# Latent attention of a two-block model: queries and keys projected straight into feature-major layout, only the rotary parts transposed

## The chip, the cores and the metric

One core of a Trainium2 chip runs the whole kernel. The metric is the device time of one execution in microseconds (us). Before the change the median of three runs is 1034.88 us (1034.77 to 1035.86).

## What is computed

The program is two transformer blocks on 256 tokens of width 1024, each with a mixer and a squared-ReLU MLP of width 4096; the second block has two layers. All weights are streamed once. The change touches one part, the latent attention of the last layer:

```
q_full = heads(rmsnorm(c_q, q_norm) @ w_uq, 8, 64 + 32)        # c_q: 256 x 384, w_uq: 384 x 768
q_nope, q_rope = q_full[..., :64], rope(q_full[..., 64:], positions)
kv_full = heads(rmsnorm(c_kv, kv_norm) @ w_ukv, 8, 64 + 64)    # c_kv: 256 x 256, w_ukv: 256 x 1024
k_nope, v_d = kv_full[..., :64], kv_full[..., 64:]
k_rope = rope(k_r[:, :, None, :], positions)[:, :, 0, :]       # one rotated key part for all 8 heads
s = (q_nope . k_nope + q_rope . k_rope) * 96 ** -0.5           # per head, then mask, softmax, @ v_d
```

The scores are a product over 96 features, so queries and keys must lie with their features on the partitions: `qTm[0:96, head, token]` and `kTm[0:96, head, token]`, rows 0 to 63 unrotated and rows 64 to 95 rotated.

## The kernel before, in words

The order on every engine is written out by hand, with semaphores between engines. TensorE (PE) runs each job's units one after the other; a unit is one weight tile of 128 x 1024 values that SyncE loads. ScalarE (ACT) rounds each unit to fp32r (`whi`, function `hi`, L1229) and VectorE (DVE) subtracts to get the rest (`wlo`, function `lo`, L1718), six units ahead of their use. A product is three matmuls, hi x hi, hi x lo and lo x hi (`three`, L445 to L447). PSUM has eight banks: jobs alternate between the pairs 0-1 and 2-3, and banks 4 to 7 (`W0` to `W3`) serve transposes and attention. A job may start only when the pair that it reuses has been emptied (`pair_free`, L470).

Jobs are of kinds. In kind "T" the activations are the stationary operand and the weights move, up to 512 columns at a time, and the result is token-major (tokens on the partitions). In kind "F" the weights are stationary and 256 tokens move, and the result is feature-major.

The stage in question has 24 units, numbered u = 0 to 23 in three loops that run in step: on PE (from L1158), on ACT (`for u in range(n3)`, L1623) and on DVE (L2344). The jobs are `sq` and `sk` (u 0 to 7), `cq` (8 to 11), `ckv` (12 to 14), `sv` (15 to 18), and then those of the latent attention:

- `uq0` (u = 19, 20) and `uq1` (u = 21): the queries, 512 and 256 columns wide, token-major, evicted by ACT into `qtk`;
- `kn` (u = 22): the unrotated keys, token-major, evicted into `kfl`, and `vn` (u = 23): the values.

Between them PE runs the last steps of another attention (`sb_sums` at L1114, `sb_values` at L1127). DVE rotates the key part in `ckt` at u = 20 and copies it eight times into `kfl` (L2404), and rotates the queries in `qtk` at u = 21 (`rotate`, L2331). PE then transposes all of `qtk` and `kfl`, per head and block of 128 tokens, in `mla_turn` (L1144, the transpose at L1153): eight transposes after u = 22, eight in the middle of u = 23, and sixteen behind it. ACT evicts each half of the heads with `ml_copy` (L1616 to L1620), 96 rows by 1024 columns, into `qTm` and `kTm`. After the loop, `out_job("wob", ...)` (L1007) interleaves the output projection with the steps of the latent attention: `out_part` 0 for the first token block, then the step (3, -1), which waits for `ml_T` (L1060 to L1062) and issues the first logits (`att_logits`, L651), then `out_part` 0 for the second block, and so on. The steps wait for one another through the softmax on DVE (L1803, L1806) and ACT (L1298). The last MLP follows.

ACT's order from u = 20 is: `sb_second(3)`, `hi(26)`, eviction of `uq0`; `sb_hi` twice, `hi(27)`, eviction of `uq1`; `hi(28)`, eviction of `kn`; `hi(29)`, `ml_copy(0)`, `ml_copy(1)`, eviction of `vn`; `ml_copy(2)`, `ml_copy(3)`; `hi(30)`. (The numbers are those of the stage's units; the code writes `base + u + LEAD`.) DVE's is: `lo(26)`, rotation of the key part and its copies; `sb_split` twice, `lo(27)`, rotation of the queries; `lo(28)`; `lo(29)`; and then the first step of the softmax.

## Time and profile before

| what | value |
|---|---|
| median of three runs | 1034.88 us |
| the profiled execution, its own time | 1035.65 us |
| its span in the trace | 1033.9 us |
| mean granted TensorE clock | 0.998 |
| PE busy | 1024.7 us, 99% of the span |
| DVE, ACT busy | 719.9 us (70%), 580.8 us (56%) |
| mean DMA rate | 179 GB/s |

The profile's page lists busy time per engine and the chain of work that ended last. The timelines list the instructions of one engine in order of time: start, duration, engine, line, operation, output and inputs, and in brackets the idle time before and what ended it. A matmul's duration is longer than its distance to the next one, because matmuls overlap; what counts for PE is the distance from start to start. PEld is PE's weight load, which runs beside the matmuls.

### The profile page before, as it was taken

Reading aid. Unit: us, or ns where it says so; the run is one execution under the profiler, and the core shown is the slowest. Engines: PE = TensorE matmul, PEld = TensorE weight load, DVE = VectorE, ACT = ScalarE, POOL = GpSimd, SP = SyncE. Lnnn points to the kernel's source line nnn. Section 1 sums busy time; section 2 is a strip of 40 time slices with the busy share of each in tenths; the row PEclk is TensorE's granted clock in tenths of the full one; section 3 lists DMA queues with packets and bytes.
Section 4 is the critical chain, followed back from the end, with each engine's and each line's share of the span. In section 5 each row is a group of like instructions: output and inputs, shape, how many; then the busy total and the mean of one; then the engine's idle time right before and its main releaser. Section 6 shows DMA issues by size and latency. Waiting matters only on the chain.

```text
span 1033.9 us, 16294 instructions
## 1 busy us (share of the span) xinstructions
PE 1024.7 (99%) x5808; PEld 878.3 (85%) x5808; DVE 719.9 (70%) x1156; ACT 580.8 (56%) x871; POOL 1.0 (0%) x8
## 2 busy tenths in 40 slices
PE   9999999999999999999999999999999999999997
PEld 8998888888888888888878888888998878888886
DVE  6898768787866556678676766665678669565663
ACT  6655675764654444464665544544569757444542
POOL 0000000000000000000000000000000000000000
PEclk9999999999999999999999999999999999999999
DMA  8855445464665667547324765665455336665541
GB/s 277 273 191 184 143 146 193 153 202 162 205 202 193 193 186 238 166 156 252 123 85 144 241 195 181 193 192 193 129 179 170 116 123 216 207 206 185 183 142 41
DMA packets 53846, 184.96 MB, mean 179 GB/s; under 512 B 6000, under 2 KB 9504, under 8 KB 53792
## 3 DMA queue, kind: packets, MB, share of 16 engines
q1 hardware_dynamic: 52736, 183.17, 54.4%
q10 hardware_dynamic: 1056, 1.06, 0.3%
q8 instruction: 35, 0.57, 0.2%
q14 instruction: 19, 0.16, 0.0%
HBM read 183.14 MB, written 1.07 MB: 178 GB/s over the span
## 4 chain that ended last, share of the span: by engine, by line
PE 95%; DVE 2%; DMA 1%; ACT 1%; issue 0%; SPq 0%; ACTq 0%; DVEq 0%
PE ps L445 18%; PE ps L446 18%; PE ps L447 18%; PE ps L923 15%; PE ps L926 8%; PE ps L487 3%; PE ps L563 3%; PE ps L490 2%; PE ps L898 2%; PE ps L651 1%; DMA raw<-stream 1%; PE ps L675 1%; PE ps L901 1%; DVE wlo L1718 1%; ACT whi L1229 0%
## 5 line engine op out<-in xcount | busy, mean ns | idle before, releaser
L1718 DVE TENSOR_TENSOR wlo<-raw,whi 128x1024 fp32r<-128x1024 f32 x338 | 409.8, 1222 | 157.7 <-ACT whi L1229 154.7
L1229 ACT ACTIVATE whi<-raw 128x1024 fp32r<-128x1024 f32 x338 | 353.1, 1056 | 176.2 <-PE ps L447 121.0
L445 PE MATMUL ps<-whi,y_hi 128*128 128x512 f32 (+1 forms) x524 | 206.3, 394 | 0.0
L446 PE MATMUL ps<-wlo,y_hi 128*128 128x512 f32 (+1 forms) x524 | 203.6, 389 | 0.0
L447 PE MATMUL ps<-whi,y_lo 128*128 128x512 f32 (+1 forms) x524 | 203.6, 389 | 0.0
L923 PE MATMUL ps<-hT,whi 128*128 128x512 f32 x696 | 173.8, 392 | 0.0
L923 PEld LDWEIGHTS ps<-hT,whi 128*128 128x128 f32 x696 | 126.3, 189 | 23.4
L447 PEld LDWEIGHTS ps<-whi,y_lo 128*128 128x128 f32 x524 | 98.4, 188 | 20.6
L445 PEld LDWEIGHTS ps<-whi,y_hi 128*128 128x128 f32 x524 | 98.5, 188 | 19.2 <-issue 0.5
L446 PEld LDWEIGHTS ps<-wlo,y_hi 128*128 128x128 f32 x524 | 98.6, 188 | 18.5
L926 PEld LDWEIGHTS ps<-hT,wlo 128*128 128x128 f32 x696 | 94.9, 190 | 6.8
L926 PE MATMUL ps<-hT,wlo 128*128 128x256 f32 x696 | 97.0, 282 | 0.0
L445 PE MATMUL ps<-whi,hT 128*128 128x512 f32 (+3 forms) x248 | 94.2, 380 | 0.1
L447 PE MATMUL ps<-whi,hT 128*128 128x512 f32 (+3 forms) x248 | 92.6, 373 | 0.0
L446 PE MATMUL ps<-wlo,hT 128*128 128x512 f32 (+3 forms) x248 | 92.6, 373 | 0.0
L1491 ACT ACTIVATE arena<-ps 128x512 f32<-128x512 f32 x48 | 28.5, 595 | 67.6 <-PE ps L926 67.5
L2151 DVE TENSOR_TENSOR arena<-ps,arena 128x512 f32<-128x512 f32 x48 | 33.2, 691 | 43.0 <-ACT arena L1491 43.0
L445 PE MATMUL ps<-hT,whi 128*128 128x256 f32 x192 | 55.4, 288 | 0.0
L445 PEld LDWEIGHTS ps<-whi,hT 128*128 128x128 f32 x248 | 46.6, 188 | 9.3 <-DVE wlo L1883 0.8
L446 PE MATMUL ps<-hT,whi 128*128 128x256 f32 x192 | 54.3, 283 | 0.0
L447 PE MATMUL ps<-hT,wlo 128*128 128x256 f32 x192 | 54.3, 283 | 0.0
L447 PEld LDWEIGHTS ps<-whi,hT 128*128 128x128 f32 x248 | 46.6, 188 | 7.9
(279 smaller groups left out, 1139.3 us busy)
## 6 DMA issues: line engine op xcount, KB each, us to landing
raw<-stream SPq DMA_DIRECT2D x338, 512.0 KB, 4.2
x<-x_in SPq DMA_DIRECT2D x2, 512.0 KB, 4.1
arena<-scratch ACTq DMA_DIRECT2D x1, 1024.0 KB, 10.7
arena<-rb SPq DMA_DIRECT2D x1, 1024.0 KB, 6.3
bm<-decay SPq DMA_DIRECT2D x1, 1024.0 KB, 6.5
out<-arena SPq DMA_DIRECT2D x2, 320.0 KB, 2.2
cst<-const SPq DMA_DIRECT2D x1, 520.0 KB, 7.7
raw<-stream SPq DMA_DIRECT2D x2, 256.0 KB, 5.2
```

Of the source, the lines that this page charges most:

```text
L445: pe.matmul(o, a[0], b[0], start=start, stop=False)
L446: pe.matmul(o, a[0], b[1], start=False, stop=False)
L447: return pe.matmul(o, a[1], b[0], start=False, stop=stop)
L487: pe.matmul(o, whi[:, u % RING, kt * P:(kt + 1) * P], hTw[:, kt, :], start=kt == 0, stop=False)
L490: m = pe.matmul(o[:, 0:S], wlo[:, u % RING, kt * P:(kt + 1) * P], hT[0][:, kt, :], start=False, stop=kt == KT - 1)
L563: return pe.transpose(o, i, cst[0:n, C_ID:C_ID + n])
L923: pe.matmul(o, whi[:, slot, kt * P:(kt + 1) * P], hTw[:, kt, :], start=kt == 0, stop=False)
L926: m = pe.matmul(o[:, 0:S], wlo[:, slot, kt * P:(kt + 1) * P], hT[0][:, kt, :], start=False, stop=kt == KT - 1)
L1229: act.activation(whi[:, u % RING, :], raw[:, u % RAW, :], ACT.Copy).then_inc(sem("hi_done"), 1)
L1491: act.activation(crossed[:, half % 2, :, :], ps[:, b:b + 2, S:2 * S], ACT.Copy).then_inc(sem("m_cross"), 1)
L1718: dve.tensor_tensor(wlo[:, u % RING, :], raw[:, u % RAW, :], whi[:, u % RING, :].bitcast(F32), ALU.subtract).then_inc(sem("lo_done"), 1)
L2151: dve.tensor_tensor(v, ps[:, b:b + 2, 0:S], crossed[:, half % 2, :, :], ALU.add).then_inc(sem("m_sum"), 1)
```

## The change

Three things are rearranged. The query projection is split into its rotated columns (`uqr`, 256 columns, token-major, u = 19) and its unrotated ones (`uqn`, 512 columns, u = 20 and 21). `uqn` and `kn` are of a new kind "N": the weights are stationary and 256 tokens move, so that they come out feature-major in four blocks of 128 features; block g holds head g in rows 0 to 63 and head g + 4 in rows 64 to 127. ACT evicts such a job in two instructions (`evac_heads`), rows 0 to 63 and rows 64 to 127, both into rows 0 to 63 of `qTm` or `kTm`. The 32 transposes of `mla_turn` go. In their place `rope_turn`, between u = 22 and u = 23, makes two transposes of `ckt` and four of `qtk` with the rotated parts; from these, ACT copies two of four row groups into rows 64 to 95 of `qTm` at u = 23, and DVE, behind `lo(29)`, copies the key part into one head, spreads it to the other seven, and copies the other two row groups. DVE's eight-fold copies at u = 20 go, and so do the four `ml_copy`. The first logits wait for `ml_T` 3 (one signal of ACT, two of DVE) and for the eviction of `kn`. The number of units, and what each loads, stays 24; `uqr` takes one where `uq1` took one, `uqn` two where `uq0` took two.

```diff
--- before.py
+++ after.py
@@ -54,8 +54,8 @@
 
     def add(name, kind, cols, nkt):
         nonlocal u, pair
-        kpu = KT if kind == "F" else min(nkt, UNIT // cols)
-        n = cols // P if kind == "F" else -(-nkt // kpu)
+        kpu = {"F": KT, "N": UNIT // (nkt * P)}.get(kind) or min(nkt, UNIT // cols)
+        n = cols // P // (kpu if kind == "N" else 1) if kind in "FN" else -(-nkt // kpu)
         jobs[name] = dict(kind=kind, cols=cols, nkt=nkt, kpu=kpu, u0=u, n=n, pair=pair % 2)
         u += n
         pair += 1
@@ -83,8 +83,8 @@
     pair += 2
     mlp(1)
     for name, kind, cols, nkt in (("sq", "F", 512, KT), ("sk", "F", 512, KT), ("cq", "T", 384, KT),
-                                  ("ckv", "T", 288, KT), ("sv", "T", 512, KT), ("uq0", "T", 512, 3),
-                                  ("uq1", "T", 256, 3), ("kn", "T", 512, 2), ("vn", "T", 512, 2)):
+                                  ("ckv", "T", 288, KT), ("sv", "T", 512, KT), ("uqr", "T", 256, 3),
+                                  ("uqn", "N", 512, 3), ("kn", "N", 512, 2), ("vn", "T", 512, 2)):
         add(name, kind, cols, nkt)
     jobs["wob"] = dict(kind="O", u0=u, n=8, pair=pair % 2)
     u += 8
...
@@ -503,6 +503,14 @@
                         if mid is not None and kt == KT // 2:
                             mid()
                         m = three(o, wsl(u, kt * P, (kt + 1) * P), X(kt), kt == 0, kt == KT - 1)
+                elif j["kind"] == "N":
+                    nkt = j["nkt"]
+                    for i in range(j["kpu"]):
+                        block = k * j["kpu"] + i
+                        o = ps[:, b + block // 2, (block % 2) * S:(block % 2 + 1) * S]
+                        for kt in range(nkt):
+                            c = (i * nkt + kt) * P
+                            m = three(o, wsl(u, c, c + P), X(kt), kt == 0, kt == nkt - 1)
                 else:
                     w = j["cols"]
                     kts = range(k * j["kpu"], min((k + 1) * j["kpu"], j["nkt"]))
@@ -1059,7 +1067,8 @@
                         pe.wait_ge(sem("evac_v"), evac_v_no["fk"])
                     if (a, n) == (3, -1):
 
-                        pe.wait_ge(sem("ml_T"), 4)
+                        pe.wait_ge(sem("ml_T"), 3)
+                        pe.wait_ge(sem("evac"), evac_no["kn"] + 1)
                     if n == 2:
 
                         pe.wait_ge(sem("evac"), evac_no[{1: "fv", 2: "bv", 3: "vn"}[a]] + 1)
@@ -1086,8 +1095,8 @@
 
 
             def lat(which):
-                def f(kt, t):
-                    c = slice(t * P, (t + 1) * P)
+                def f(kt, t=None):
+                    c = slice(0, S) if t is None else slice(t * P, (t + 1) * P)
                     return latent[which][0][:, kt, c], latent[which][1][:, kt, c]
                 return f
 
...
@@ -1141,43 +1150,37 @@
                     if p % 2:
                         m.then_inc(sem("sb_v"), 1)
 
-            def mla_turn(src, c0, parts=(0, 1)):
-
-                for h4 in parts:
-                    if c0 >= 2:
-
-                        pe.wait_ge(sem("ml_T"), c0 + h4 - 1)
-                    for h in range(4 * h4, 4 * h4 + 4):
-                        for t in range(TT):
-                            o = ps[0:96, W0 + 2 * h4 + (h % 4) // 2, (h % 2) * S + t * P:(h % 2) * S + (t + 1) * P]
-                            m = pe.transpose(o, src[:, t, 96 * h:96 * h + 96], cs(C_ID))
-                    m.then_inc(sem("ml_tr"), 1)
-
-            seq = [(n, k) for n in ("sq", "sk", "cq", "ckv", "sv", "uq0", "uq1", "kn", "vn")
+            def rope_turn():
+
+                pe.wait_ge(sem("sb_lo"), 2)
+                pe.wait_ge(sem("ro_k"), 1)
+                for t in range(TT):
+                    m = pe.transpose(ps[0:96, W2, t * P:(t + 1) * P], ckt[:, t, 192:288], cs(C_ID))
+                m.then_inc(sem("ml_tr"), 1)
+                pe.wait_ge(sem("ro_q"), 2)
+                for g in range(2):
+                    for t in range(TT):
+                        m = tr(ps[:, W0 + g, t * P:(t + 1) * P], qtk[:, t, g * P:(g + 1) * P])
+                m.then_inc(sem("ml_tr"), 1)
+
+            seq = [(n, k) for n in ("sq", "sk", "cq", "ckv", "sv", "uqr", "uqn", "kn", "vn")
                    for k in range(JOBS[n]["n"])]
             for u, (name, k) in enumerate(seq):
-                if k == 0 and name in ("uq0", "kn"):
-
-                    pe.wait_ge(sem("la_lo"), 1 if name == "uq0" else 2)
-                X = {"uq0": lat(0), "uq1": lat(0), "kn": lat(1), "vn": lat(1)}.get(name, h_all)
+                if k == 0 and name in ("uqr", "kn"):
+
+                    pe.wait_ge(sem("la_lo"), 1 if name == "uqr" else 2)
+                X = {"uqr": lat(0), "uqn": lat(0), "kn": lat(1), "vn": lat(1)}.get(name, h_all)
 
                 def between():
 
                     if u == 3:
                         spread_rs(2)
-                    if u == 23:
-                        pe.wait_ge(sem("ro_q"), 2)
-                        mla_turn(qtk, 0, (1,))
-
                 if u == 0:
                     first_units(2, seq[0:3])
                 if u >= 3:
                     unit(name, k, X, between)
                 if u == 22:
-
-                    pe.wait_ge(sem("sb_lo"), 2)
-                    pe.wait_ge(sem("ro_q"), 1)
-                    mla_turn(qtk, 0, (0,))
+                    rope_turn()
                 if u in SB_SCORES:
                     if u == 8:
                         pe.wait_ge(sem("evac_v"), evac_v_no["sk"] - 1)
@@ -1201,9 +1204,6 @@
                         for t in range(TT):
                             m = tr(ps[:, b, col + t * P:col + (t + 1) * P], (cqt, ckt)[c][:, t, kt * P:(kt + 1) * P])
                     m.then_inc(sem("la_tr"), 1)
-            pe.wait_ge(sem("ro_k"), 1)
-            pe.wait_ge(sem("evac"), evac_no["kn"] + 1)
-            mla_turn(kfl, 2)
             out_job("wob", 5, 3, steps_cd, len(seq))
             mlp(2)
 
@@ -1239,8 +1239,6 @@
                     src = ps[:, b:b + 2, :].rearrange("p a (b c) -> p (a b) c", b=2)[:, 0:n, :]
                 else:
                     src = ps[:, b:b + 2, 0:j["cols"]]
-                if name == "kn":
-                    src = src.rearrange("p t (h n) -> p t h n", h=8)
                 if rows is not None:
 
                     act.wait_ge(sem("n_rs"), rows)
@@ -1248,6 +1246,14 @@
                     act.activation(dst[:, 1, :], src[:, 1, :], func, scale=rs[:, 1:2]).then_inc(sem("evac"), 1)
                     return
                 act.activation(dst, src, func, scale=scale).then_inc(sem("evac"), 1)
+
+            def evac_heads(name, dst, scale):
+
+                b = 2 * pair_of[name]
+                act.wait_ge(sem("used"), last_unit(name) + 1)
+                src = ps[:, b:b + 2, :].rearrange("p a (b c) -> p (a b) c", b=2)
+                act.activation(dst[0:64, 0:4, :], src[0:64, :, :], ACT.Copy, scale=scale)
+                act.activation(dst[0:64, 4:8, :], src[64:P, :, :], ACT.Copy, scale=scale).then_inc(sem("evac"), 1)
 
             def wide_cross(name, h):
                 n, _, crossed_half, to = wide_part(name, h)
@@ -1569,9 +1575,9 @@
             norm(3, 1, base + 32 + LEAD)
             mlp(1)
             base = JOBS["sq"]["u0"]
-            L3 = {"cq": cqt, "ckv": ckt, "sv": sv, "uq0": qtk[:, :, 0:512], "uq1": qtk[:, :, 512:768],
-                  "kn": kfl.rearrange("p t (h n) -> p t h n", h=8)[:, :, :, 0:64], "vn": vnt}
-            ends = {last_unit(n): n for n in L3}
+            L3 = {"cq": cqt, "ckv": ckt, "sv": sv, "uqr": qtk[:, :, 0:256], "vn": vnt}
+            L3_heads = {"uqn": (qTm, 96.0 ** -0.5), "kn": (kTm, 1.0)}
+            ends = {last_unit(n): n for n in (*L3, *L3_heads)}
             n3 = JOBS["wob"]["u0"] - base
 
             def sb_first(p):
@@ -1612,13 +1618,6 @@
                     m = act.activation(latent[c][0][:, kt, :], ps[:, b, col:col + S], ACT.Copy,
                                        scale=sml[:, G_LAT[c] + kt:G_LAT[c] + kt + 1])
                 m.then_inc(sem("la_hi"), 1)
-
-            def ml_copy(c):
-                dst, scale = (qTm, 96.0 ** -0.5) if c < 2 else (kTm, 1.0)
-                act.wait_ge(sem("ml_tr"), c + 1)
-                h, b = 4 * (c % 2), W0 + 2 * (c % 2)
-                act.activation(dst[0:96, h:h + 4, :], ps[0:96, b:b + 2, :].rearrange("p a (b c) -> p (a b) c", b=2),
-                               ACT.Copy, scale=scale).then_inc(sem("ml_T"), 1)
 
             for u in range(n3):
                 if u == 2:
@@ -1644,19 +1643,24 @@
                 else:
                     hi(base + u + LEAD)
                 if u == 23:
-                    ml_copy(0)
-                    ml_copy(1)
+
+                    act.wait_ge(sem("ml_tr"), 2)
+                    for i in range(2):
+                        m = act.activation(qTm[64:96, i::4, :], ps[32 * i:32 * i + 32, W0:W0 + 2, 0:S], ACT.Copy,
+                                           scale=96.0 ** -0.5)
+                    m.then_inc(sem("ml_T"), 1)
                 if base + u in ends:
                     n = ends[base + u]
-                    evac(n, L3[n], rows=2 if n in ("cq", "ckv", "sv") else None)
+                    if n in L3_heads:
+                        evac_heads(n, *L3_heads[n])
+                    else:
+                        evac(n, L3[n], rows=2 if n in ("cq", "ckv", "sv") else None)
                 if u == 6:
                     act.wait_ge(sem("ro_a"), 1)
                     act.activation(rot, rot, ACT.Sin).then_inc(sem("ro_s"), 1)
                     act.preload_act_table_set("natural_log_exp_and_others")
                 if u in (12, 15):
                     la_squares(0 if u == 12 else 1)
-            ml_copy(2)
-            ml_copy(3)
             for u in range(n3, n3 + 4):
                 steps(steps_cd, u, 0)
                 hi(base + u + LEAD)
@@ -2398,18 +2402,25 @@
                     dve.tensor_scalar(r64, ang, 3.1415925, -3.1415925, ALU.min, ALU.max).then_inc(sem("ro_a"), 1)
                 if u == 20:
                     dve.wait_ge(sem("ro_s"), 1)
-                    k8 = kfl.rearrange("p t (h n) -> p t h n", h=8)
-                    link(rotate(ckt[:, :, 256:272].unsqueeze(2), ckt[:, :, 272:288].unsqueeze(2), 1))
-                    for t in range(TT):
-                        m = dve.tensor_copy(k8[:, t, :, 64:96], ckt[:, t, 256:288].unsqueeze(1).to_broadcast([P, 8, 32]))
-                    m.then_inc(sem("ro_k"), 1)
+                    rotate(ckt[:, :, 256:272].unsqueeze(2), ckt[:, :, 272:288].unsqueeze(2), 1).then_inc(sem("ro_k"), 1)
                 if u == 21:
-                    q8 = qtk.rearrange("p t (h n) -> p t h n", h=8)
+                    q8 = qtk[:, :, 0:256].rearrange("p t (h n) -> p t h n", h=8)
+                    dve.wait_ge(sem("evac"), evac_no["uqr"] + 1)
+                    dve.wait_ge(sem("ro_k"), 1)
                     for half in range(2):
-
-                        dve.wait_ge(sem("evac"), evac_no[f"uq{half}"] + 1)
                         h = slice(4 * half, 4 * half + 4)
-                        rotate(q8[:, :, h, 64:80], q8[:, :, h, 80:96], 4, 512 * half).then_inc(sem("ro_q"), 1)
+                        rotate(q8[:, :, h, 0:16], q8[:, :, h, 16:32], 4, 512 * half).then_inc(sem("ro_q"), 1)
+                if u == 23:
+
+                    dve.wait_ge(sem("ml_tr"), 1)
+                    link(dve.tensor_copy(kTm[64:96, 0, :], ps[64:96, W2, 0:S]))
+                    dve.tensor_copy(kTm[64:96, 1:8, :],
+                                    kTm[64:96, 0, :].unsqueeze(1).to_broadcast([32, 7, S])).then_inc(sem("ml_T"), 1)
+                    dve.wait_ge(sem("ml_tr"), 2)
+                    for i in range(2, 4):
+                        m = dve.tensor_scalar(qTm[64:96, i::4, :], ps[32 * i:32 * i + 32, W0:W0 + 2, 0:S], 96.0 ** -0.5,
+                                              None, ALU.mult)
+                    m.then_inc(sem("ml_T"), 1)
 
             for u in range(n3, n3 + 4):
                 steps(steps_cd, u, 0)
@@ -2484,6 +2495,9 @@
 
     k, cols = w.shape
     w = w.reshape(k // P, P, cols)
+    if kind == "N":
+        w = w.reshape(k // P, P, cols // P // kpu, kpu, P).transpose(2, 1, 3, 0, 4).reshape(cols // P // kpu, P, -1)
+        return np.pad(w, ((0, 0), (0, 0), (0, UNIT - w.shape[2])))
     if kind == "F":
         return np.ascontiguousarray(w.reshape(k // P, P, cols // P, P).transpose(2, 1, 0, 3)).reshape(cols // P, P, -1)
     n = -(-(k // P) // kpu)
...
@@ -2510,8 +2529,8 @@
         "fq": b[:, 0:512], "fk": b[:, 512:1024], "fv": b[:, 1024:1536], "fa": np.pad(b[:, 1536:1544], ((0, 0), (0, 120))),
         "bq": b[:, 1544:2056], "bk": b[:, 2056:2568], "bv": b[:, 2568:3080],
         "sq": c[:, 0:512], "sk": c[:, 512:1024], "sv": c[:, 1024:1536], "cq": c[:, 1536:1920],
-        "ckv": c[:, 1920:2208], "uq0": a["w_uq_2"][0][:, 0:512], "uq1": a["w_uq_2"][0][:, 512:768],
-        "kn": ukv[:, :, 0:64].reshape(256, 512), "vn": ukv[:, :, 64:128].reshape(256, 512),
+        "ckv": c[:, 1920:2208], "uqr": np.ascontiguousarray(uq[:, :, 64:96]).reshape(384, 256),
+        "uqn": by_halves(np.ascontiguousarray(uq[:, :, 0:64])), "kn": by_halves(np.ascontiguousarray(ukv[:, :, 0:64])), "vn": ukv[:, :, 64:128].reshape(256, 512),
         "wo0": a["w_out"][0][:, 0:512], "wo1": a["w_out"][0][:, 512:1024],
     }
     by_group = a["w_up_attn"][0].reshape(2, 4, 64, D).transpose(1, 0, 2, 3)
```

## Rows read from the trace of the kernel before

**Rows 1.** The page, busy time, and the chain that ended last.

```profile
PE 1024.7 (99%) x5808; PEld 878.3 (85%) x5808; DVE 719.9 (70%) x1156; ACT 580.8 (56%) x871; POOL 1.0 (0%) x8
...
PE 95%; DVE 2%; DMA 1%; ACT 1%; issue 0%; SPq 0%; ACTq 0%; DVEq 0%
```

**Rows 2.** Waits ahead of weight loads, 740 to 835 us.

```profile
PEld ps L651 <- ACT arena L1620: 0.2, 1, 0.2
```

**Rows 3.** Timeline of PE, 780 to 832 us: start, duration, instruction.

```profile
794.49 0.48 PE L445 MATMUL ps<-whi,y_hi 128*128 128x512 f32 x1
...
797.34 0.33 PE L1120 MATMUL ps<-y_hi,y_lo 128*128 128x384 f32 x1
...
798.41 0.48 PE L445 MATMUL ps<-whi,y_hi 128*128 128x512 f32 x1
...
799.96 2.82 PE L1137 MATMUL ps<-bm,arena 128*64 128x256 f32 x32
802.71 0.39 PE L445 MATMUL ps<-whi,y_hi 128*128 128x256 f32 x1
...
804.96 0.40 PE L445 MATMUL ps<-whi,hT 128*128 128x512 f32 x1
...
807.71 1.03 PE L1153 MATMUL ps<-cst,arena 128*96 128x128 f32 x8
808.50 0.48 PE L445 MATMUL ps<-whi,hT 128*128 128x512 f32 x1
808.82 0.39 PE L446 MATMUL ps<-wlo,hT 128*128 128x512 f32 x1
...
812.23 1.91 PE L1153 MATMUL ps<-cst,arena 128*96 128x128 f32 x16
813.89 0.48 PE L445 MATMUL ps<-whi,y_hi 128*128 128x512 f32 x1
...
815.37 1.11 PE L651 MATMUL ps<-arena 96*128 96x128 f32 x8
```

**Rows 4.** Timeline of ACT, the same stretch.

```profile
803.32 1.05 ACT L1229 ACTIVATE whi<-raw 128x1024 fp32r<-128x1024 f32 x1
805.16 0.60 ACT L1250 ACTIVATE arena<-ps 128x512 f32<-128x512 f32 x1 [0.79 <-PE ps L447]
...
807.91 1.02 ACT L1250 ACTIVATE arena<-ps 128x1024 f32<-128x1024 f32 x1 [1.20 <-PE ps L447]
808.83 1.05 ACT L1229 ACTIVATE whi<-raw 128x1024 fp32r<-128x1024 f32 x1
...
813.35 1.93 ACT L1620 ACTIVATE arena<-ps 96x1024 f32<-96x1024 f32 x2
```

**Rows 5.** Timeline of DVE, the same stretch.

```profile
804.40 1.23 DVE L1718 TENSOR_TENSOR wlo<-raw,whi 128x1024 fp32r<-128x1024 f32 x1 [0.23 <-ACT whi L1229]
805.55 0.28 DVE L2337 TENSOR_TENSOR arena<-arena 128x128 f32<-128x128 f32 x1
...
808.22 1.22 DVE L1718 TENSOR_TENSOR wlo<-raw,whi 128x1024 fp32r<-128x1024 f32 x1
```

**Rows 6.** Groups by line and shape on ACT: count, busy, mean ns.

```profile
L1320 ACT ACTIVATE arena<-ps 128x512 f32<-128x512 f32 x18 | 10.8, 597 | 16.9 <-PE ps L563 16.7
...
L1620 ACT ACTIVATE arena<-ps 96x1024 f32<-96x1024 f32 x4 | 4.0, 1016 | 0.3 <-PE ps L1153 0.3
```

**Rows 7.** Groups by line and shape on DVE, the same columns.

```profile
L2297 DVE TENSOR_SCALAR arena<-ps 128x384 f32<-128x384 f32 x8 | 4.1, 552 | 0.3 <-PE ps L1110 0.3
...
L2042 DVE TENSOR_SCALAR arena<-arena 128x1024 f32<-128x1024 f32 x1 | 0.7, 693 | 0.0
...
L2404 DVE COPY arena<-arena 128x256 f32<-128x256 f32 x2 | 0.5, 292 | 0.0
```

**Rows 8.** Stretches at the end: busy per engine, granted clock, DMA.

```profile
1028.40:1029.40 1.00, 0.00 (x0) 0.00 (x0) 0.77 (x5) 0.81 (x3) 0.00 (x0) 1.00 0.00 0
...
1029.90:1030.40 0.50, 0.00 (x0) 0.00 (x0) 0.43 (x3) 0.43 (x1) 0.00 (x0) 1.00 0.00 0
```

More of the change, by code:

```diff
@@ L299, in model @@
         mix_no = {f"u{b}{half}": 2 * i + half for i, b in enumerate(BRANCHES) for half in range(2)}
-        emptied = [n for n in JOBS if JOBS[n]["kind"] in "TF" and not n.startswith("wo") and n not in by_vector
+        emptied = [n for n in JOBS if JOBS[n]["kind"] in "TFN" and not n.startswith("wo") and n not in by_vector
                    and n not in mix_no and n not in WIDE]
@@ L461, in _ @@
                     pairs.append((n, ("mixed", mix_no[n] + 1) if mix_no[n] < 2 else ("up_ok", mix_no[n] - 1)))
-                elif k in "TF":
+                elif k in "TFN":
                     pairs.append((n, ("evac", evac_no[n] + 1) if n in emptied else None))
@@ L2502, in layout, with by_halves @@
     ukv = a["w_ukv_2"][0].reshape(256, 8, 128)
+    uq = a["w_uq_2"][0].reshape(384, 8, 96)
+    def by_halves(v):
+        return np.ascontiguousarray(v.reshape(-1, 2, 4, 64).transpose(0, 2, 1, 3)).reshape(-1, 512)
     mats = {
@@ L2525, in layout @@
     for name, j in JOBS.items():
-        if j["kind"] in "TF":
+        if j["kind"] in "TFN":
             parts.append(units_of(mats[name], j["kind"], j["kpu"]))
```

## The prediction

> **What bounds the kernel now.** I read the page first: PE is busy for 99% of the span, and 95% of the chain that ended last is PE [rows 1]. So a transpose taken off PE is worth its time, unless PE then waits for something. The second view is the waits ahead of PE's weight loads in this stage: the first logits of the latent attention waited 0.2 us for the last `ml_copy` on ACT [rows 2]. That is small, but it says that ACT was finishing just as PE arrived: weight loads start ahead of their matmuls, and the last of the `ml_copy` pair, begun at 813.35, ended 813.35 + 1.93 = 815.28 [rows 4] against the first logits at 815.37 [rows 3]. PE, ACT and DVE meet at this point within 0.1 us. So the third view is the timelines of the three engines side by side from u = 19 on [rows 3 to 5], to see which of them arrives last once PE's work shrinks. The margin of "no change" is 0.2%, about what a measurement of this kernel can tell, or 2.07 us; the whole question lies near that size.
>
> **PE's work.** The distance from start to start gives a 256-column product: 18 matmuls of `uq1` from 802.71 to 804.96, 2.25 us, of which about 0.10 is the restart behind the other attention, so 0.120 each. Twelve 512-column ones of `kn` take 804.96 to 807.71, 0.229 each [rows 3]. Before: 18 x 0.229 + 18 x 0.120 + 12 x 0.229 = 9.03 us. After: `uqr` 18, `uqn` 36 and `kn` 24, all of 256 columns, 78 x 0.120 = 9.36. That is +0.33: the same columns, in 30 more instructions.
> Transposes: eight took 807.71 to 808.50, another eight in `vn` the same, sixteen 812.23 to 813.89 [rows 3]: 0.79 + 0.79 + 1.66 = 3.24, and each of the three groups made the next matmul late by 0.09 (808.50 to 808.82 is 0.32, not 0.23) [rows 3], 3.51 in all. The six new ones cost 6 x 0.10 + 0.09 = 0.69. So -2.82. With +0.33 it is **-2.49 us** of PE work. This would be 0.24% if nothing else came up.
>
> **PE's new clock**, from the same start of u = 19 at 794.49. Each unit of 18 takes 2.16 + 0.10 for the restart. `uqr` ends 796.75; `sb_sums` takes 1.07 (797.34 to 798.41), to 797.82; the first unit of `uqn` to 800.08; `sb_values` 2.75 (799.96 to 802.71), to 802.83; the second unit to 805.09; `kn`, 24 x 0.120 = 2.88, to 807.97 [rows 3]. The two key transposes end at 808.2. Then PE waits for the rotated queries. DVE rotated them from 805.55 to 808.22 [rows 5], behind `lo(27)` and the splits that follow `sb_values`, which ends 0.12 later now. So they are ready at about 808.4: a wait of 0.3 us with the signal. (The eight-fold copies that go from DVE lie ahead of the splits, which wait for ACT; that saves nothing.) Four transposes more, to 808.95; `vn`, 2.75 + 0.09, to 811.8; `out_part` 0 for one block, 6 x 0.229, to **813.2**. Here PE would issue the first logits, 2.2 us before the 815.37 of now [rows 3].
>
> **What is late next.** The operands of these logits. ACT first. An eviction starts 0.20 after PE's next unit starts (805.16 against 804.96, 807.91 against 807.71) [rows 3, 4]; `uqn` is thus evicted from 805.29. The evictions of 1024 columns took 1.02 us each, 0.92 to the next start (807.91 to 808.83) [rows 4]. `evac_heads` has two instructions of 64 rows with those 1024 columns. Does half the rows halve the time? No: 96 rows took 1.016 [rows 6], the same as 128. So a job's eviction costs twice as much as before, 0.95 + 0.95 from start to next start. `uqn` to 807.2; `hi(28)`, 0.95, to 808.15; `kn`, whose product is in at 807.97 + 0.20, from 808.17 to 810.05; `hi(29)`, 1.05 [rows 4], to 811.1. Before, `hi(29)` began at 808.83 [rows 4]; it is now 1.2 later. ACT's two query copies of 512 columns, 0.6 each [rows 6], run 811.0 to 812.2 and are not last; the eviction of `vn` follows and is used far later.
> DVE: `lo(29)` waits for `hi(29)` and takes 1.2 [rows 5], 811.1 to 812.25. Its own new work is queued behind it although the transposes have been ready since 808.95. The copy of the key part from PSUM, 32 rows by 256: 0.552 for 384 columns [rows 7] less 128 at about 1.04 ns a column is 0.42. Then the spread to seven heads, 32 rows by 1792, SBUF to SBUF. The price per column: 1024 in 0.693, 256 in 0.292, both on 128 rows [rows 7], slope 0.52 ns, so 0.693 + 768 x 0.00052 = 1.09. Nothing shows DVE's time to fall with fewer rows, and I take none. Then two copies of 512 columns from PSUM, 0.552 + 0.13 = 0.69 each [rows 7]. With 0.08 of overlap from instruction to instruction, except behind the link: 0.42 + 0.03 + 1.02 + 0.61 + 0.69 = **2.8 us**, to 815.05. PE's matmul starts some 0.09 behind the signal, as now (815.28 to 815.37): **815.15**.
>
> So PE arrives 2.2 us early and waits 1.9. The path is now `kn` on PE, two evictions and `hi(29)` on ACT, `lo(29)` and four copies on DVE. Everything behind the first logits (softmax steps, `hi(30)`, `lo(30)`) follows them in the order of before, and the next bank pairs are free in time (eviction of `kn` at 810.1, of `vn` at about 813). Loads are not touched: same units, same bytes; SP's and POOL's queues have nothing moved. The sum is 815.15 - 815.37 = **-0.2 us**. Against the profiled execution, 1035.65 with a span of 1033.9, it gives 1035.4; this one lies 0.8 above the median of the runs, and against the median it is 1034.7.
>
> **The unknown prices.** Two have no row. First, the spread copy reads one head of 256 columns seven times and writes 1792 in a row. The fast slope comes from copies with an even count of repeats (eight in L2404) or one run [rows 7]. Upper end: one element a cycle, as the PSUM rows show, 0.552 + 1408 x 0.00104 = 2.0 us, 0.9 more. I take 1.09, since both the shape and the memory are nearer to L2404.
> The Trainium skill ("VectorE: DVE Perf Modes", What auto-detection actually checks) speaks against this: the double rate for one source within SBUF needs outermost counts that are both even or equal. Seven repeats against one run of 1792 would fail, seven against seven would pass; no row here has an odd count. By its rule in the worse reading the sum would be +0.7 in place of -0.2.
> Second, moving rows: ACT reads rows 64 to 127 and writes 0 to 63; DVE and ACT move 32-row groups. No copy from one row to another stands in the trace. Lower end: the straight price, which I take, because an instruction's time has not depended on its rows. Upper end: double. Below the straight price there is no reason to go.
> The wait itself: can it cost more than its 1.9 us? At the end of the kernel PE's last matmul is over before 1028.4, and two us later, until 1030.4, the granted clock still is 1.00, the 2.4 GHz level [rows 8]. So no loss of clock is priced.
>
> **The rivals.**
> (a) *The forecast*, -0.2 us, 1034.7: chance 0.50.
> (b) *The spread copy at one element a cycle.* The logits start at 816.05, +0.7, 1035.6. For: the odd count, above. Against: the fast eight-fold copy. 0.30.
> (c) *The work saved on PE comes through.* If DVE and ACT were ready at 813.2, the gain would be 2.2 us, or 2.5 without the wait for the rotation: 1032.4 to 1032.7. It needs 64- and 32-row instructions to cost far less than full ones, ACT's in proportion (-0.9 for `kn`, -0.5 at least for `uqn`) and DVE's copies as well. The 96-row row speaks against it. 0.09.
> (d) *Slower: the moves across rows cost double.* The second instruction of each `evac_heads` takes 2.0: `uqn` until 808.2, `hi(28)` 809.15, `kn` 812.1, `hi(29)` 813.1, `lo(29)` 814.3, then 2.8 + 0.7 for the one DVE copy that moves rows: 817.8, and the logits at 817.9, +2.5, 1037.4. It decides from a price of about 1.8 times the straight one. No row is for it, only the absence of one against. 0.06.
> The rest, 0.05, is a change in the alignment of code or loads somewhere in a kernel 99% PE.
> That the change doesn't do what it says (transposes going, but not from PE's path) I can exclude: they are on PE, and PE is the chain.
>
> **The numbers.** The likeliest gives 1034.7. (a) and (b) hold 0.80 of the chance and lie within 0.2% of 1034.88; with partial forms of (c) and (d) "same" is 0.81. Faster by over 2.07 us needs almost all of (c): 0.11. Slower 0.08, from (d) or (b) with half of (d). The range goes from 1032.6, nearly the whole of (c), to 1036.4, which takes in (b), half of (d)'s extra and the spread of the runs shown (up to 1035.86).
>
> **What the profile after would show.** 1153-like transposes gone, six in one place near 808 to 809; 256-column matmuls at 0.12 in `uqn` and `kn`. Four ACT evictions of 64 x 1024 at 1.0 us each. `hi(29)` about 1.2 us later than now. The spread copy at 1.1 us (at 2.0 it is (b)). And ahead of the first L651 matmul an idle PE of 1.9 us, put down to DVE, where there was 0.2 put down to ACT. A PE idle below 0.5 us there would prove the chain wrong; so would logits that start before 814.5 or behind 816.5 on this scale.

## The result, and the profile after

The changed kernel takes 1038.45 us, the median of eleven runs (1036.15 to 1038.91), against 1034.96 of before, also of eleven. The ratio of the means is 1.0027 with a 95% interval of 1.002 to 1.0035: slower by 0.27%, and between the medians 3.5 us, 0.34%. The eleven runs are not one heap. Two stand at 1036.15 and 1036.25 with a mean granted TensorE clock of 0.999; nine lie from 1037.50 to 1038.91 with 0.995 to 0.998. The profiled execution took 1037.97 us with a span of 1036.2.

The page after, busy time and the chain that ended last, against [rows 1]:

```profile
span 1036.2 us, 16304 instructions
...
PE 1022.9 (99%) x5812; PEld 877.3 (85%) x5812; DVE 722.9 (70%) x1158; ACT 580.3 (56%) x871; POOL 1.0 (0%) x8
...
PE 94%; DVE 2%; DMA 1%; ACT 1%; issue 1%; SPq 0%; ACTq 0%; DVEq 0%
```

PE's busy time fell by only 1.8 us although 2.5 us of work went, and the span grew by 2.3. The waits ahead of PE's weight loads, over the whole run, name the place, against [rows 2]:

```profile
PEld ps L659 <- DVE arena L2421: 3.6, 1, 3.6
...
PEld ps L571 <- DVE arena L2346: 0.4, 1, 0.4
```

The first logits (L659 is the old L651) waited 0.2 us for ACT before; now it is 3.6 us, for the last instruction of DVE's block. (That is the idle time of the weight loads, which run ahead; the matmuls themselves stand still for the 3.19 us of the timeline below.) The second row is the wait for the rotated queries. PE's timeline through the stage, against [rows 3] (the rows at 807.69 and 808.21 are the six new transposes):

```profile
794.19 0.36 PE L445 MATMUL ps<-whi,y_hi 128*128 128x256 f32 x1
...
796.41 0.34 PE L1129 MATMUL ps<-y_hi,y_lo 128*128 128x384 f32 x1
...
807.69 0.38 PE L1158 MATMUL ps<-cst,arena 128*96 128x128 f32 x2
808.21 0.66 PE L571 MATMUL ps<-cst,arena 128*128 128x128 f32 x4
808.62 0.48 PE L445 MATMUL ps<-whi,hT 128*128 128x512 f32 x1
...
812.59 0.39 PE L447 MATMUL ps<-whi,y_lo 128*128 128x512 f32 x1
816.17 1.84 PE L659 MATMUL ps<-arena 96*128 96x128 f32 x8 [3.19 <-DVE arena L2421]
...
818.23 0.63 PE L446 MATMUL ps<-wlo,y_hi 128*128 128x512 f32 x1
818.66 0.63 PE L447 MATMUL ps<-whi,y_lo 128*128 128x512 f32 x1
...
820.15 1.03 PE L659 MATMUL ps<-arena 96*128 96x256 f32 x4
...
821.48 0.39 PE L447 MATMUL ps<-whi,y_lo 128*128 128x512 f32 x1
```

The stage begins 0.30 us earlier on this profile's scale than on the other (794.19 against 794.49), with the same program ahead of it. From there: the last matmul before the logits starts at 812.59, as the prediction had it (it put their end at 813.2, less 0.3), and the logits at 816.17, which is 816.47 on the scale of the other profile, just inside the 816.5 behind which the prediction would have called its chain wrong. Behind them something else is wrong: 512-column matmuls follow one another at 0.43 us (818.23 to 818.66), not 0.23 as at 821.48. The stretches say why. Each row gives the length, the busy time of PE, PEld, DVE, ACT and POOL, and then the granted clock:

```profile
813.00:815.00 2.00, 0.00 (x0) 0.00 (x0) 2.00 (x2) 1.25 (x2) 0.00 (x0) 1.00 0.76 225
815.00:816.00 1.00, 0.00 (x0) 0.00 (x0) 0.99 (x2) 0.00 (x0) 0.00 (x0) 1.00 0.19 74
816.00:816.50 0.50, 0.33 (x2) 0.33 (x3) 0.11 (x1) 0.00 (x0) 0.00 (x0) 0.96 0.00 0
...
818.00:819.00 1.00, 1.00 (x4) 0.80 (x3) 0.93 (x8) 0.00 (x0) 0.00 (x0) 0.50 0.00 0
819.00:820.00 1.00, 1.00 (x4) 0.74 (x3) 0.17 (x1) 0.79 (x4) 0.00 (x0) 0.56 0.02 8
820.00:821.00 1.00, 1.00 (x7) 0.86 (x5) 0.00 (x0) 0.86 (x6) 0.00 (x0) 1.00 0.00 0
```

PE does nothing from 813.0 to 816.17. The granted clock falls to 0.50, the 1.2 GHz level, at about 816.46 (that is where the mean of 0.96 over 816.0 to 816.5 puts it), when PE has just begun again, and stays there until about 819.9. The two effects account for the profile to a tenth. The logits are late by 816.17 - (815.37 - 0.30) = 1.1 us. From the first to the third group of logits it takes 6.2 us (816.17 to 822.40, the next group behind the rows shown) against 4.7 before, 1.5 more. 1.1 + 1.5 less the 0.3 of the start is 2.3, the growth of the span.

ACT and DVE in the same stretch, against [rows 4] and [rows 5]:

```profile
808.04 1.02 ACT L1255 ACTIVATE arena<-ps 64x1024 f32<-64x1024 f32 x1
809.07 1.02 ACT L1256 ACTIVATE arena<-ps 64x1024 f32<-64x1024 f32 x1
810.00 1.04 ACT L1229 ACTIVATE whi<-raw 128x1024 fp32r<-128x1024 f32 x1
```

```profile
808.07 1.22 DVE L1722 TENSOR_TENSOR wlo<-raw,whi 128x1024 fp32r<-128x1024 f32 x1
811.08 1.23 DVE L1722 TENSOR_TENSOR wlo<-raw,whi 128x1024 fp32r<-128x1024 f32 x1 [1.79 <-ACT whi L1229]
812.33 0.42 DVE L2416 COPY arena<-ps 32x256 f32<-32x256 f32 x1
812.79 2.01 DVE L2417 COPY arena<-arena 32x1792 f32<-32x1792 f32 x1
814.73 1.39 DVE L2421 TENSOR_SCALAR arena<-ps 32x512 f32<-32x512 f32 x2
```

ACT evicts each feature-major job in two instructions of 1.02 us; the first two rows are those of `kn`. `hi(29)`, the row at 810.00, starts 1.2 us later than before by the two profiles' own scales, 1.5 us when the 0.30 between them is allowed for. `lo(29)` follows at 811.08, and behind it stands DVE's block: 0.42, then 2.01 for the spread copy, then 1.39 for two.

### The profile page after: what moved, and what is told of

It reads as the page before. It is cut to its first block, busy times and chain, and to the rows that moved or that the text cites. A ratio compares the mean times of both kernels' runs of the same rounds, so it can differ in the third digit from the quotient of the medians.

```text
span 1036.2 us, 16304 instructions
## 1 busy us (share of the span) xinstructions
PE 1022.9 (99%) x5812; PEld 877.3 (85%) x5812; DVE 722.9 (70%) x1158; ACT 580.3 (56%) x871; POOL 1.0 (0%) x8
## 4 chain that ended last, share of the span: by engine, by line
PE 94%; DVE 2%; DMA 1%; ACT 1%; issue 1%; SPq 0%; ACTq 0%; DVEq 0%
PE ps L445 18%; PE ps L446 18%; PE ps L447 18%; PE ps L931 15%; PE ps L934 8%; PE ps L487 3%; PE ps L571 3%; PE ps L490 2%; PE ps L906 2%; PE ps L659 1%; DMA raw<-stream 1%; PE ps L683 1%; PE ps L909 1%; DVE wlo L1722 1%; ACT whi L1229 0%
## 5 line engine op out<-in xcount | busy, mean ns | idle before, releaser
L445 PE MATMUL ps<-whi,y_hi 128*128 128x512 f32 (+1 forms) x518 | 204.2, 394 | 0.0
L447 PE MATMUL ps<-whi,y_lo 128*128 128x512 f32 (+1 forms) x518 | 201.4, 389 | 0.0
L934 PE MATMUL ps<-hT,wlo 128*128 128x256 f32 x696 | 97.0, 282 | 0.0
L445 PE MATMUL ps<-whi,hT 128*128 128x512 f32 (+3 forms) x244 | 92.5, 379 | 0.1
L447 PE MATMUL ps<-whi,hT 128*128 128x512 f32 (+3 forms) x244 | 91.0, 373 | 0.0
L445 PE MATMUL ps<-hT,whi 128*128 128x256 f32 x200 | 57.6, 288 | 0.0
L446 PE MATMUL ps<-hT,whi 128*128 128x256 f32 x200 | 56.6, 283 | 0.0
L447 PE MATMUL ps<-hT,wlo 128*128 128x256 f32 x200 | 56.5, 283 | 0.0
```

The lines of the kernel that those rows point to most:

```text
L445: pe.matmul(o, a[0], b[0], start=start, stop=False)
L446: pe.matmul(o, a[0], b[1], start=False, stop=False)
L447: return pe.matmul(o, a[1], b[0], start=False, stop=stop)
L934: m = pe.matmul(o[:, 0:S], wlo[:, slot, kt * P:(kt + 1) * P], hT[0][:, kt, :], start=False, stop=kt == KT - 1)
```

## Experiments

Theory 1, formed on this: the cost has two parts. PE waits for a chain of `kn`'s two evictions, `hi(29)`, `lo(29)` and DVE's block, whose spread copy runs at 1.04 ns a column; and the idle time makes PE's clock fall in most executions. Rivals: the spread of the runs comes from loads or code placement; another wait would take the place of any that is removed; the copies are slow because they touch 32 rows or repeat their source. All experiments start from the changed kernel. They were run in three groups, each on a chip of its own: E1 to E4, E5 to E8, E9 and E10. "Before" was run beside each group and took 1034.88, 1035.08 and 1034.94 us, so runs of different groups are compared by their distance from the "before" beside them.

**E1, the idle time filled.**

```diff
                     if (a, n) == (3, -1):
+                        for _ in range(24):
+                            pe.matmul(ps[:, W3, 0:S], hT[0][:, 7, 0:P], hT[0][:, 6, :], start=True, stop=True)
                         pe.wait_ge(sem("ml_T"), 3)
```

> The changed kernel, with 24 extra matmuls of 256 columns into bank 7 ahead of the wait for the first logits (they change nothing that is read: the bank is cleared before its next use). PE now idles 3.2 us there; the 24 matmuls take 24 x 0.12 = 2.9 us of that. Theory 1 (the wait for DVE costs about 1.1 to 1.3 us, and what is above it is TensorE's clock falling to 1.2 GHz during the idle time): the logits start at the same time, the granted clock stays 1.00, and the runs lie together near 1036.2, none near 1038.8. Rival (the spread of the changed kernel's runs from 1036.2 to 1038.9 has another cause, loads or code placement): the runs spread as before, up to 1038.9, or move up by the matmuls' time.

Measured: 1035.99 us, eleven runs from 1035.80 to 1036.17. PE's timeline there:

```profile
812.32 3.03 PE L1071 MATMUL ps<-hT 128*128 128x256 f32 x24
815.67 1.16 PE L659 MATMUL ps<-arena 96*128 96x128 f32 x8 [0.32 <-DVE arena L2423]
```

24 matmuls that compute nothing, put into a wait, made the kernel 2.4 us faster (it was 3.5 us above before and is 1.1 above), and its runs agree within 0.4 us. PE still waits for DVE at the end of them. So the wait costs 1035.99 - 1034.88 = 1.1 us, and what the changed kernel has above that, 3.5 - 1.1 = 2.4 us in the median, is clock.

**E2, DVE's block ahead of `lo(29)`.**

```diff
-                if u == 23:
+                if u == 22:
                     dve.wait_ge(sem("ml_tr"), 1)
                     link(dve.tensor_copy(kTm[64:96, 0, :], ps[64:96, W2, 0:S]))
```

> The changed kernel, with DVE's block of four copies moved ahead of lo(29), behind lo(28). Theory 1: the block then runs 809.3 to 813.1 while ACT still evicts kn (until 810.1), and the logits start near 813.2, just behind PE's arrival at 812.8. 3.0 us earlier than in the changed kernel and 1.9 earlier than before: 1033.1, granted clock 1.00, faster than before. Rival (lo(29), which is then 3 us later, or ACT's doubled evictions, take over the wait): 1035 to 1036.

Measured: 1033.09 us (1032.88 to 1033.57), ratio 0.9983 (0.9974 to 0.9992). DVE's block and PE's first logits:

```profile
809.37 0.42 DVE L2416 COPY arena<-ps 32x256 f32<-32x256 f32 x1
809.83 2.01 DVE L2417 COPY arena<-arena 32x1792 f32<-32x1792 f32 x1
811.76 1.39 DVE L2421 TENSOR_SCALAR arena<-ps 32x512 f32<-32x512 f32 x2
```

```profile
813.20 1.16 PE L659 MATMUL ps<-arena 96*128 96x128 f32 x8 [0.17 <-DVE arena L2421]
```

The block itself is as long as before; only its place in the queue changed, and one character of source is worth 5.3 us: the changed kernel is 3.5 us above before, this one 1.8 below. `lo(29)` came 2.1 us later than there (813.18 against 811.08) and nobody waited for it. The rival falls.

**E3, the spread in even counts.**

```diff
-                    link(dve.tensor_copy(kTm[64:96, 0, :], ps[64:96, W2, 0:S]))
-                    dve.tensor_copy(kTm[64:96, 1:8, :],
-                                    kTm[64:96, 0, :].unsqueeze(1).to_broadcast([32, 7, S])).then_inc(sem("ml_T"), 1)
+                    link(dve.tensor_copy(kTm[64:96, 0:2, :], ps[64:96, W2, 0:S].unsqueeze(1).to_broadcast([32, 2, S])))
+                    dve.tensor_copy(kTm[64:96, 2:8, :],
+                                    kTm[64:96, 0, :].unsqueeze(1).to_broadcast([32, 6, S])).then_inc(sem("ml_T"), 1)
```

> The changed kernel, with the key part copied from PSUM to two heads at once (512 columns, 0.69 us instead of 0.42) and spread from there to six heads instead of seven. Theory 1 with the rule on even and odd counts: 1536 columns at the double rate take about 0.96 us instead of 2.01, so the block is 0.8 us shorter, the logits start at 815.4 and PE idles 2.4 us, short enough for the clock to stay at 1.00: 1035.3, and the runs lie together. Rival (copies of 32 rows, or with a repeated source, run at one element a cycle whatever the count): 1.7 us for the spread, logits within 0.1 us of the changed kernel's, and the runs spread as there.

Measured: 1036.68 us, from 1035.05 to 1037.68. DVE's two copies, and PE's first logits with the idle time ahead of them:

```profile
812.14 0.69 DVE L2416 COPY arena<-ps 32x512 f32<-32x512 f32 x1
812.86 0.95 DVE L2417 COPY arena<-arena 32x1536 f32<-32x1536 f32 x1
```

```profile
815.18 1.16 PE L659 MATMUL ps<-arena 96*128 96x128 f32 x8 [2.40 <-DVE arena L2421]
```

The copies did what was expected: 0.95 us for six repeats against 2.01 for seven. But I had expected 2.4 us of idle time to be harmless, and that is wrong: four of the eleven runs are at 1035.05 to 1035.48, seven at 1036.57 to 1037.68. The mean clocks are 0.998 and 0.999 in the four, 0.996 to 0.998 in the seven. This profile happens to be one of the four. E9 settles what the seven are.

**E4, the spread done twice.** The same spread copy is put in once more ahead of the one that is there, and DVE waits for the first to end before it starts the second.

> The changed kernel, with the spread copy done twice: DVE's block is 2.0 us longer and PE idles 5.2 us. Theory 1: every execution loses the clock; 2.0 us for the wait and the whole loss of clock each time: above 1040.5, with a granted clock of 0.995 or below in all runs. Rival (no clock loss from idle time): 1036.2 to 1038.9 plus 2.0 with the same spread and some runs at 0.999.

Measured: 1040.03 us, four runs from 1039.36 to 1040.78, less than the 1040.5 that I expected; clocks 0.995, 0.995, 0.996 and one of 0.998, where I expected none above 0.995. Stretches of its profile:

```profile
812.00:815.00 3.00, 0.74 (x4) 0.28 (x2) 2.90 (x4) 1.99 (x3) 0.00 (x0) 0.95 0.52 173
815.00:816.00 1.00, 0.00 (x0) 0.00 (x0) 1.00 (x1) 0.00 (x0) 0.00 (x0) 0.50 0.01 4
...
821.00:822.00 1.00, 1.00 (x4) 0.75 (x4) 0.19 (x3) 0.74 (x4) 0.00 (x0) 0.73 0.03 8
```

PE's last matmul before the wait is over near 812.7 (0.74 us busy in the first row). The mean of 0.95 over 812 to 815 means that the clock had already fallen at about 814.7, two us into the idle time, and it came back only near 821.5, 3.5 us after PE had begun again at 817.98. With 2.0 us of further wait on E1's 1036.0, a run that kept its clock would take 1038.0; the four lie 1.4 to 2.8 us above that. No run escaped, the one at 0.998 lost least.

**E5 and E6, towards the best version.** E5 is E2 with E3's edit. E6 moves the rotation too:

```diff
+                if u == 20:
+                    dve.wait_ge(sem("ro_s"), 1)
+                    rotate(ckt[:, :, 256:272].unsqueeze(2), ckt[:, :, 272:288].unsqueeze(2), 1).then_inc(sem("ro_k"), 1)
+                if u == 20:
+                    q8 = qtk[:, :, 0:256].rearrange("p t (h n) -> p t h n", h=8)
...
                 if u not in SB_SCORES and u not in (14, 17):
                     lo(base + u + LEAD)
```

> E2's earlier block together with E3's even spread. Theory 1: the block now ends near 812.4, before PE arrives at 812.8, so the 0.2 to 0.3 us left in E2 ahead of the first logits goes: 1032.8, granted clock as before the change. Rival (what is left is PE's own restart, not the wait): within 0.1 us of E2's 1033.1.

> E5, and the rotation of keys and queries moved ahead of lo(26), into the time in which DVE waits for hi(26). That takes away PE's wait of 0.4 us between the key and the query transposes. Theory: 1032.4, 2.5 us faster than before, the whole of the PE work saved. Rival (lo(26), lo(27) or the splits become late instead, by up to 2 us): PE waits in front of sb_values' followers or the transposes, 1032.8 or more.

Measured: E5 1032.58 us (1032.29 to 1033.04), E6 1032.49 (1031.99 to 1033.23), ratios to before 0.9976 (0.9966 to 0.9986) and 0.9975 (0.9966 to 0.9984). E5's logits follow PE's last matmul with no idle time, and it is 2.5 us below before where E2 is 1.8; its rival, that PE's own restart was left, falls. E6's transposes and first logits on PE:

```profile
807.63 0.38 PE L1158 MATMUL ps<-cst,arena 128*96 128x128 f32 x2
807.85 0.60 PE L571 MATMUL ps<-cst,arena 128*128 128x128 f32 x4
...
812.42 1.05 PE L659 MATMUL ps<-arena 96*128 96x128 f32 x8
```

PE doesn't stand idle here: the query transposes follow those of the key at once, where the changed kernel left a gap (807.69 to 808.21). The gap's 0.4 us show in the profile, but between the medians of E5 and E6 there is 0.1, which this measurement can't tell from nothing. E6 is 2.6 us faster than before, all of the 2.5 us that leave PE.

**E7, one eviction instruction in place of two**, with 16 of E1's matmuls. The second `act.activation` of `evac_heads` is left out, so heads 4 to 7 of the unrotated queries and keys are missing from the computation.

> The changed kernel with only the first of the two instructions of each evac_heads, so that heads 4 to 7 of the unrotated queries and keys are left out, and with 16 extra matmuls as in E1, to keep the clock out of it. Theory 1 (ACT's doubled eviction is a link of the chain): hi(29) and lo(29) come 1.0 us earlier, the logits start 1.0 us earlier than in E1: 1035.0. Rival (only DVE's own block matters, behind the transposes): no change from E1's 1036.0.

Measured: 1035.28 us (1034.90 to 1035.92), 0.2 us above the "before" beside it, where E1 is 1.1 above the one beside it: 0.9 less. ACT and PE:

```profile
807.94 1.02 ACT L1257 ACTIVATE arena<-ps 64x1024 f32<-64x1024 f32 x1 [0.91 <-PE ps L447]
808.87 1.05 ACT L1231 ACTIVATE whi<-raw 128x1024 fp32r<-128x1024 f32 x1
```

```profile
812.87 2.07 PE L1071 MATMUL ps<-hT 128*128 128x256 f32 x16
815.04 1.16 PE L659 MATMUL ps<-arena 96*128 96x128 f32 x8
```

`hi(29)` starts at 808.87, not at 810.00, and the logits at 815.04. In the profile the whole 1.1 us arrives there, and 0.9 of it in the medians. E7 also leaves out the second instruction for `uqn`; that lets the eviction of `kn` start some 0.16 us earlier (807.94 against 808.04, with this profile's transposes 0.06 later than the changed kernel's), and the rest is the second eviction of `kn`. So the doubled eviction is a link of the chain, worth about a microsecond.

**E8, the price of copies.** Six copies into scratch behind DVE's block (`one` is head 0's 256 columns on rows 64 to 95):

```diff
+                    link(dve.tensor_copy(c3(kflat[r, 0:5 * S], a=5), one.to_broadcast([32, 5, S])))
+                    link(dve.tensor_copy(c3(kflat[r, 0:6 * S], a=6), one.to_broadcast([32, 6, S])))
+                    link(dve.tensor_copy(c3(kflat[r, 0:5 * S], a=5), kTm[r, 1:6, :]))
+                    link(dve.tensor_copy(c3(kflat[r, 0:5 * 260], a=5)[:, :, 0:S], one.to_broadcast([32, 5, S])))
+                    link(dve.tensor_copy(c3(kflat[0:32, 0:5 * S], a=5), kTm[r, 1:6, :]))
+                    link(dve.tensor_copy(c3(kflat[:, 0:5 * S], a=5), cst[:, 0:S].unsqueeze(1).to_broadcast([P, 5, S])))
```

> Six extra copies on DVE behind its block, each into scratch: (i) 5 repeats of 256 into one run of 1280, (ii) 6 repeats into one run of 1536, (iii) 1280 straight into 1280, (iv) 5 repeats into 5 rows with gaps, (v) as (iii) but from rows 64 to 95 to rows 0 to 31, (vi) as (i) on 128 rows. If the rule is that the outermost counts must both be even or be equal: (ii), (iii), (v) and (iv) run at 0.52 ns an element (0.96, 0.82, 0.82, 0.82 us), (i) and (vi) at 1.04 (1.5 us). If repeats of an odd count are slow in themselves, (iv) takes 1.5 as well. If moves across rows cost more, (v) is slower than (iii).

Measured in one execution, which took 1043.93 us at a mean clock of 0.993 (the six hold up the softmax on DVE, for which PE waits another 3.1 us, so the kernel's time prices no copy); the six in order:

```profile
816.19 1.47 DVE L2427 COPY arena<-arena 32x1280 f32<-32x1280 f32 x1
817.69 0.95 DVE L2428 COPY arena<-arena 32x1536 f32<-32x1536 f32 x1
818.68 0.82 DVE L2429 COPY arena<-arena 32x1280 f32<-32x1280 f32 x1
819.53 0.95 DVE L2430 COPY arena<-arena 32x1280 f32<-32x1280 f32 x1
820.51 0.81 DVE L2431 COPY arena<-arena 32x1280 f32<-32x1280 f32 x1
821.36 1.49 DVE L2432 COPY arena<-cst 128x1280 f32<-128x1280 f32 x1
```

Five repeats into one run take 1.47 us for 1280 columns, about the 1.04 ns a column of the spread copy; six take 0.95 for 1536; a straight copy 0.82; from rows 64 to 95 to rows 0 to 31 no more, 0.81; and 128 rows cost what 32 do, 1.49. Five repeats into five separate rows take 0.95. I had expected 0.82. It is neither rate. An estimate fits: three of the five rows at 1.04 ns a column are 0.80 us, and with the 0.15 that is left of the straight copy (0.82 less 1280 columns at 0.52 ns) it is 0.95, as if the work were split into three rows and two. No run tests that reading.

**E9, E3 with its idle time filled**, and **E10, E1 with E6's rotation.**

> E3 with 16 of the extra matmuls of E1 (1.9 us) ahead of the wait. If the upper half of E3's runs (1036.6 to 1037.7) is lost clock, filling the idle 2.4 us takes it away and leaves the logits where they are: 1035.1, all runs within 0.5 us of one another. Rival (E3's spread comes from loads or code placement): median 1036 or above, spread of 2 us.

> E1 with the rotation moved ahead of lo(26), as in E6, and nothing else. Theory: PE's wait of 0.4 us for the rotated queries goes, but the first logits still wait for the chain of kn's evictions, hi(29), lo(29) and DVE's block, which starts from kn and not from the transposes: 1036.0, as E1. Rival (PE's 0.4 us are on the path): 1035.6.

Measured: E9 1035.35 us (1035.19 to 1036.06). The heap at 1036.6 to 1037.7 is gone, and the level is that of E3's four lower runs; 0.25 above what I expected. The eleven runs lie within 0.9 us, not the 0.5 that I expected; "before" itself, beside them, spreads over 1.5. So E3's upper seven had lost clock, to an idle time of 2.4 us. E10 1036.13 us (1035.96 to 1036.79), 1.2 us above the "before" beside it, against 1.1 of E1: PE's earlier transposes buy nothing while the chain through `kn` sets the logits, as expected. The same edit is not harmful in E6, and not needed before the rest is mended.

## Why the prediction was wrong

**PE's work**: right. -2.49 us was the sum, and E6, in which nothing waits, is 2.6 faster than before. The 18 products of `uqr` took 794.19 to 796.41, 2.22 us where 2.26 were forecast. **PE's new clock** was right to a tenth in every row: the transposes' wait of 0.3 us is 0.4, the end of `vn` and of the first `out_part` is where it was put.

**What is late next**: the place and the order were right, two evictions on ACT, `hi(29)`, `lo(29)`, DVE's block, and PE in front of the first logits. The wait was forecast at 1.9 us and is 3.2. On the common scale the logits were forecast at 815.15 - 0.30 = 814.85 and came at 816.17, 1.3 late. The spread copy is 0.92 of it. The rest lies ahead of the block, which starts at 812.33 and not at 811.95: the second instruction of an eviction starts 1.03 behind the first, not 0.95, and the hand-overs between engines add up.

**The spread copy** is the first step that failed, and the smaller: "I take 1.09, since both the shape and the memory are nearer to L2404." It measured 2.01, the upper end, rival (b). L2404 had eight repeats and this one seven, and that difference, which I named, decided. E8 and E3 show that it is the count: 5 into a run 1.47 us, 6 into a run 0.95, on the same rows, engine and memory. The rule of the Trainium skill ("VectorE: DVE Perf Modes", What auto-detection actually checks), outermost counts both even or equal, agrees with every copy here except in degree: for equal odd counts, 0.95 in place of 0.82. It should have had the greater chance, since it was the only evidence on odd counts.

**The clock** is the second, and the larger: "So no loss of clock is priced." I had read [rows 8] as two us of idle time at full clock and taken that for a general allowance. It was one occasion, and the same trace shows its end. PE's last matmul is over at 1027.43, and the clock falls right behind the rows that I used:

```profile
1027.40:1028.40 1.00, 0.03 (x1) 0.00 (x0) 0.97 (x4) 0.51 (x2) 0.00 (x0) 1.00 0.01 2
...
1030.40:1030.90 0.50, 0.00 (x0) 0.00 (x0) 0.38 (x1) 0.48 (x1) 0.00 (x0) 0.66 0.00 0
1030.90:1031.40 0.50, 0.00 (x0) 0.00 (x0) 0.00 (x0) 0.14 (x1) 0.00 (x0) 0.50 0.00 0
```

So the trace of before held a loss of clock by idle time, some 3.1 us behind the last matmul, and the prediction gave it neither a term nor a chance. The time at which it falls differs from profile to profile: two us into the idle time in E4, 3.5 us behind PE's stop in the changed kernel, and E3's profile kept it through 2.4 us, while by their times seven of E3's eleven runs lost it. The range (up to 1036.4) was just wide enough for the two fastest runs, 1036.15 and 1036.25, which kept the clock: they are rival (b)'s 1035.6 and the 0.4 us ahead of the block. It had nothing for the lost clock of the other nine. Had all runs kept it, E1's 1036.0 would have stood inside the range, for the reasons of (b). In my list the slower rival was (d), moves across rows at twice the price. That did not happen: the two evictions take 1.02 each, straight or across, and E8's crossing copy 0.81 against 0.82.

The sum as it came out: -2.5 of work, + 3.6 of waits (0.4 and 3.2), which is +1.1 for the chain, and in the median +2.4 for the clock (3.5 less 1.1). Against the forecast of 1034.7 the 3.7 us that are missing are the logits' 1.3 and the clock's 2.4. Unknown remains what decides in a single execution whether the clock is lost and how much of it: the same program gives both.

## What to carry to other kernels

Where an engine is 99% busy and its partners just keep up, taking work off it moves the wait to the partners; put the partner's new instructions ahead of those in its queue that are needed last, as E2 did with one number. Price idle time on TensorE twice, once as a wait and once as a chance to lose the clock, and if it can't be removed, fill it. When a copy repeats its source an odd number of times into one run, split off one repeat.

## What the runs showed of the hardware

- TensorE's clock fell to the 1.2 GHz level with idle times of 2.4 us (in seven of E3's eleven runs, by their times), 3.2 us (nine of the changed kernel's eleven) and 5.2 us (all four of E4); with the 0.2 us of E2 no run shows it, nor with a wait filled with matmuls (E1, E9). In the rows at 0.50, 512-column products follow at 0.43 us against 0.23. One loss cost 1.3 to 2.8 us (the runs above the level of E1, of E3's four fast ones and of E4's 1038.0).
- An instruction on ACT costs by its columns, not its rows: 64 x 1024 took 1.02 us as 128 x 1024 does, on the same rows or moved by 64.
- A DVE copy in SBUF, fp32: 0.52 ns a column, straight or with six or eight repeats (0.82 us for 1280, 0.95 for 1536), 1.04 with five or seven repeats into one run (1.47 us for 1280, 2.01 for 1792), and in between (0.95 us for 1280) with five into five separate rows. 32 or 128 rows make next to no difference (1.47 and 1.49), nor do other rows for the result (0.81).
